# Attention weights of the differential heads turned outside TensorE, in one layer of a hybrid encoder

## The reference

```python
h = rmsnorm(x, pre_g);  P = h @ w_in          # 1024 x 3328
# A: 8 query heads, 2 key/value heads, width 64, window of 128 keys, a sink per head, ALiBi
# B: 4 heads, each with two softmax maps over keys of width 64, values of width 128
for i in range(8):                            # query blocks of 128
    s = q[i] @ k[: i + 1].T / 8 - slope * dist      # both maps, masked by chunks of 64
    p = softmax(s);  attn = p[0] - lam * p[1]
    o[i] = attn @ v[: i + 1]
o = rmsnorm(o, subln_g) * (1 - lambda_init)
y = concat(A * silu(gA), B * silu(gB)) @ w_out
out = x + rmsnorm(y, post_g)
```

## Time and profile before

| what | value |
|---|---|
| runs of before | 507.57 us median of 3 (507.13 to 507.67) |
| profiled execution | 508.39 us, span 506.6 us |
| PE busy | 499.1 us, 99% of the span, 2724 matmuls |
| DVE, ACT, POOL busy | 282.2, 244.6, 104.0 us |
| granted TensorE clock, mean | 0.996 |
| DMA | 35.19 MB, mean 69 GB/s |

### The profile page before, as it was taken

How to read it: one execution, slowest core, us unless ns; L and a number is a source line. 1 busy time by engine, 2 the same in 40 slices (tenths; PEclk the granted TensorE clock), 3 DMA queues, 4 the chain that set the end, 5 groups by cost and what they waited for, 6 DMA issues and landing times.

```text
span 506.6 us, 7438 instructions
## 1 busy us (share of the span) xinstructions
PE 499.1 (99%) x2724; PEld 420.5 (83%) x2724; DVE 282.2 (56%) x682; ACT 244.6 (48%) x555; POOL 104.0 (21%) x131
## 2 busy tenths in 40 slices
PE   8999999999999999999999999999999999999995
PEld 7999988888888888888887777788888888888884
DVE  3969743565656555455467576654763593333432
ACT  6952643555545546546466665633652462222211
POOL 1070522223032022203034335312303000000000
PEclk9999999999999999999999999999999999999998
DMA  8910141120151012211011130111000925322222
GB/s 277 308 50 0 43 123 41 25 59 0 43 124 44 1 43 55 71 42 42 1 42 43 42 85 1 42 43 41 2 1 0 251 82 155 136 83 85 83 85 82
DMA packets 43701, 35.19 MB, mean 69 GB/s; under 512 B 19025, under 2 KB 36881, under 8 KB 43665
## 3 DMA queue, kind: packets, MB, share of 16 engines
q1 hardware_dynamic: 41216, 30.52, 21.6%
q10 hardware_dynamic: 2448, 4.20, 2.2%
HBM read 26.88 MB, written 4.19 MB: 61 GB/s over the span
## 4 chain that ended last, share of the span: by engine, by line
PE 95%; issue 2%; DMA 1%; ACT 0%; SPq 0%; DVE 0%; POOLq 0%; POOL 0%; DVEq 0%; ACTq 0%
PE proj L1282 46%; PE scores L1396 15%; PE scores L1212 8%; PE scores L1307 7%; PE banks L1329 7%; PE banks L1319 3%; PE scores L1354 2%; PE banks L1374 2%; PE banks L1362 1%; PE banks L1212 1%; PE proj L1212 1%; DMA wv_raw<-in_w_in 1%; PE banks L1338 1%; PE banks L1243 0%; PE banks L1254 0%
## 5 line engine op out<-in xcount | busy, mean ns | idle before, releaser
L702 POOL TENSOR_TENSOR w_lo<-w_raw,w_hi 128x256 fp32r<-128x256 f32 x84 | 63.5, 786 | 175.9 <-ACT w_hi L780 175.9
L1282 PE MATMUL proj<-hT_hi,w_lo 128*128 128x512 f32 x336 | 90.0, 401 | 0.0
L1282 PE MATMUL proj<-hT_hi,w_hi 128*128 128x512 f32 x336 | 89.1, 399 | 0.0
L1282 PE MATMUL proj<-hT_lo,w_hi 128*128 128x512 f32 x336 | 88.7, 400 | 0.0
L1282 PEld LDWEIGHTS proj<-hT_hi,w_hi 128*128 128x128 f32 x336 | 61.0, 188 | 12.7 <-issue 0.4
L1282 PEld LDWEIGHTS proj<-hT_hi,w_lo 128*128 128x128 f32 x336 | 60.5, 188 | 13.2 <-issue 1.9
L1282 PEld LDWEIGHTS proj<-hT_lo,w_hi 128*128 128x128 f32 x336 | 60.6, 188 | 11.8 <-issue 0.8
L1111 DVE CUSTOM_DVE_ANT_0 weights<-scores,dist_b 128x128 f32<-128x128 f32 (+7 forms) x64 | 45.9, 754 | 43.9 <-PE scores L1307 43.9
L859 ACT ACTIVATE weights<-weights,small 128x128 f32<-128x128 f32 (+7 forms) x64 | 49.0, 768 | 17.5 <-DVE small L1111 17.4
L869 ACT ACTIVATE weightsT<-banks 128x512 f32<-128x512 f32 (+3 forms) x48 | 23.6, 492 | 60.7 <-PE banks L1319 60.7
L706 POOL TENSOR_TENSOR small<-small 128x4 f32<-128x4 f32 (+2 forms) x17 | 14.1, 829 | 160.8 <-DVE small L1191 108.3
(11 more groups left out here) (126 smaller groups left out, 735.1 us busy)
## 6 DMA issues: line engine op xcount, KB each, us to landing
w_raw<-in_w_in SPq DMA_DIRECT2D x13, 512.0 KB, 3.8
w_raw<-in_w_in SPq DMA_DIRECT2D x16, 256.0 KB, 3.6
x_res<-in_x SPq DMA_DIRECT2D x8, 512.0 KB, 4.4
out<-y_out ACTq DMA_DIRECT2D x14, 256.0 KB, 2.3
x_all<-in_xT SPq DMA_DIRECT2D x6, 512.0 KB, 8.1
k_stack<-k_stack SPq DMA_DIRECT2D x12, 256.0 KB, 3.7
wo_raw<-in_w_out SPq DMA_DIRECT2D x8, 256.0 KB, 5.3
wo_raw<-in_w_out SPq DMA_DIRECT2D x4, 512.0 KB, 9.9
```

The lines of the kernel that those rows point to most:

```text
L702: nc.gpsimd.tensor_tensor(w_lo[:, n % SPLIT, k], w_raw[:, n % RAW, k], w_hi[:, n % SPLIT, k].bitcast(F32), ALU.subtract).then_inc(w_lo_rea ...
L1282: last = nc.tensor.matmul(to, w[:, slot, k, :], h[:, k, HALF * half:HALF * half + HALF], start=(p == 0 and k == first), stop=(p == PIECES ...
```

## The change

The turn of the B weights leaves PE. After `b_mix` DVE transposes the 32x32 blocks of the mixed weights in place (`b_turn`). SP writes the result to a buffer in DRAM, waits until it has landed, and reads it back in four DMAs, one for each group of 32 partitions; the DRAM layout does the rest of the turn. So that the pieces are contiguous, the keys stand in another order in scores, weights and distances: all first quarters of the key blocks, then all second ones, and so on (`by_group`); the scores' matmuls read `k_stack` in runs of 32 keys. The ACT copies and `weightsT` go; there are three buffers of mixed weights instead of two.

`b_values` has v as the stationary operand and the turned weights, in runs of 32, as the moving one; it comes two slots after the scores instead of one, and in its slot after all but two of the pieces (`AFTER_VALUES`). Its result stands turned already. ACT copies the bank to `out_B` (`b_out`); for the norm PE turns four blocks back (`b_back`), ACT squares them, DVE and POOL make the root as before. SP writes the 512 factors to DRAM (`b_spread_out`) and reads them back into all partitions (`b_spread_in`), and DVE scales `out_B` in place (`b_finish`). These stages come one slot apart; in the remaining pieces, every fourth piece.

In A, the scores of the next step come directly behind the values of the one before, in the same slot. The row of 1024 norm factors goes to DRAM and back into all partitions by two DMAs of SP, and ACT puts it in order; the diagonals and their product go. One slot is added at the end, and the last slots hold 17 pieces instead of 12, so that 14 remain behind them.

```diff
-                 + [4, 7, 7, 6, 3, 6, 5, 5] + [6, 1, 5])
-SCORES_FIRST = {1, 2, 3, 10, 11, 17, 18}
-PIECE_BETWEEN = {8, 16, 36}
-PIECE_AHEAD = {37}
+                 + [4, 7, 7, 6, 3, 6, 5, 5] + [8, 4, 3, 2])
+PIECES_AHEAD = {8: 1, 16: 1, 36: 1, 37: 1}
+AFTER_VALUES = 2
...
+            turns[n + 1] = unit[1]        # an A step
+            due[n + 2] = unit[1]          # a B unit
...
-            steps.append(("b_mix", last[1]))
+            steps += [("b_mix", last[1]), ("b_turn", last[1])]
...
+            if slot in due:
+                ahead = 1 if kind == "a" else max(1, count - AFTER_VALUES)
+                take(ahead)
+                count -= ahead
+                values(due[slot])
...
+            steps.append(("a_values", turning))
+            if kind == "a" and now + 1 < STEPS_A:
+                steps += [("a_weights", 2 * now + 1), ("a_scores", now + 1)]
...
+        for at_end in ending:
+            f, stage = at_end
+            steps += [[], [("b_back", f), ("b_square", f), ("b_root", f)], [("b_spread_out", f)],
+                      [("b_spread_in", f)], [("b_finish", f)]][stage]
+            at_end[1] += 1
...
     while at < len(pieces):
         take(1)
         vector_parts()
+        for at_end in ending:
+            f, stage = at_end
+            if at % 4 == 0:
+                steps += [...][stage]
+                at_end[1] += 1
...
             load_w(1)
+            sp.wait_ge(x_scaled, 1)
+            sp.dma_start(scales[:, :], x_scale).then_inc(scales_stored, 16)
+            sp.wait_ge(scales_stored, 16)
+            sp.dma_start(scale_spread..., scales...to_broadcast([P, SEQ])).then_inc(scales_loaded, 16)
...
+            def turn(u):
+                blocks = u % TILES + 1
+                width = GROUP * blocks
+                if u >= 2:
+                    sp.wait_ge(b_turned[u % 2], 64 * (u // 2))
+                sp.wait_ge(b_blocks_turned, u + 1)
+                sp.dma_start(turn_store[u % 2, :, :, 0:width].rearrange("g p x -> p g x"),
+                             by_group(weights_of(u), blocks)).then_inc(b_turn_stored, 16)
+                sp.wait_ge(b_turn_stored, 16 * (u + 1))
+                for g in range(4):
+                    sp.dma_start(by_group(weights_of(u)[GROUP * g:GROUP * (g + 1)], blocks),
+                                 turn_store[u % 2, g, :, 0:width].rearrange("(q k) x -> k q x", q=4)
+                                 ).then_inc(b_turned[u % 2], 16)
...
+                elif step == "b_spread_out":
+                    sp.wait_ge(b_rooted, f + 1)
+                    sp.dma_start(spread_store[:, :], rms_b).then_inc(b_spread_stored, 16)
+                elif step == "b_spread_in":
+                    sp.wait_ge(b_spread_stored, 16 * (f + 1))
+                    sp.dma_start(on_b..., spread_store...to_broadcast([P, HALF])).then_inc(b_spread, 16)
...
-            for t in range(TILES):
-                nc.vector.tensor_scalar(diagonals[:, P * t:P * t + P], ident[:, :], x_scale[:, t:t + 1], None,
-                                        ALU.mult).then_inc(diagonals_made, 1)
...
+                    nc.vector.transpose(w, w).then_inc(b_blocks_turned, 1)
...
-                        nc.tensor.matmul(scale_rows[:, cols], ones[:, :], diagonals[:, cols],
-                                         start=True, stop=True).then_inc(scale_spread, 1)
...
-                    pe.wait_ge(turned_read, turned_count("b_transpose", u, (blocks - 1) // 4))
+                    pe.wait_ge(b_turned[u % 2], 64 * (u // 2 + 1))
...
-                        last = nc.tensor.matmul(mixed[:, P * (u % 4):P * (u % 4) + P], weightsT[:, b, :],
-                                                v_sb[:, b, P * head:P * head + P],
+                        last = nc.tensor.matmul(to, v_sb[:, b, P * head:P * head + P], turned_block(u, b),
```

More of the change, by code:

```diff
@@ L34 @@
 CHUNK, HEAD_DIM = 64, 64
+GROUP = 32
 EPS = 1e-6
@@ L145, in make_schedule, with values @@
     place = {unit: n for n, unit in enumerate(order)}
-    turns = {}
+    turns, due = {}, {}
     for unit, n in place.items():
-        turns.setdefault(n + 1, []).insert(0, unit)
+        if unit[0] == "a":
+            turns[n + 1] = unit[1]
+        else:
+            due[n + 2] = unit[1]
+    def values(u):
+        steps.append(("b_values", u))
+        if u % 4 == 3:
+            steps.append(("b_out", u // 4))
+            ending.append([u // 4, 0])
+    ending = []
     steps += [("split", 0), ("split", 1)]
@@ L152, in make_schedule @@
     vector_parts()
-    for slot in range(len(order) + 3):
+    for slot in range(len(order) + 4):
         kind, now = order[slot] if slot < len(order) else (None, None)
@@ L168, in make_schedule @@
             vector_parts("store_low")
-        if finishing:
-            steps.append(("b_finish", before[1] // 4))
-        turning = sorted(turns.get(slot, []))
-        first = [("b_transpose", unit, 0) if which == "b" else ("a_transpose", 2 * unit)
-                 for which, unit in turning[:1]]
-        if kind == "b":
-            assert {("kB", now // TILES), ("qB", now // TILES)} <= set(UNITS[:at // (2 * PIECES)])
-            first.append(("b_scores", now))
-        elif kind == "a":
-            first.append(("a_scores", now))
@@ L179, in make_schedule @@
-        if slot in SCORES_FIRST:
-            first.reverse()
-        if slot in PIECE_AHEAD:
-            take(1)
-            count -= 1
-        steps += first[:1]
-        if slot in PIECE_BETWEEN and len(first) == 2:
-            take(1)
-            count -= 1
-        steps += first[1:]
-        vector_parts()
-        for n, (which, unit) in enumerate(turning):
-            if n:
-                steps.append(("b_transpose", unit, 0))
-            if which == "b" and unit % TILES >= 4:
-                if n or kind is None:
-                    take(1)
-                    count -= 1
-                steps.append(("b_transpose", unit, 1))
-            if kind == "b" and n == len(turning) - 1:
+        ahead = PIECES_AHEAD.get(slot, 0)
@@ L231, in make_schedule @@
             vector_parts("store_low")
-        if finishing:
-            steps.append(("b_finish_transpose", before[1] // 4))
+        for at_end in ending:
[3 more added lines that the diff above has]
+            at_end[1] += 1
+        ending = [at_end for at_end in ending if at_end[1] < 5]
         take(max(0, count))
@@ L1064, in _ @@
                     if kind == "gB":
-                        dve.wait_ge(turned_read, turned_count("b_finish_transpose", 2 * head + half))
+                        dve.wait_ge(b_finished, 2 * head + half + 1)
                     else:
```

250 lines of the change are left out of this document (131 added, 119 removed).

## The result

The changed kernel takes 522.81 us (median of 4 runs, 521.67 to 523.01), the kernel before beside it 507.62 (4 runs, 507.13 to 507.98); ratio 1.0299, 95% interval 1.0286 to 1.0312. The profiled execution took 522.7 us with a span of 520.9. Forecast were 509.4 us, range 497 to 522. The direction was the likelier one of the two, the size was not: 15 us are lost, 2 were forecast, and the time lies 0.8 us above the range.

The account below looks back on a forecast made before the run. PE was taken as the bound, busy 499.1 of 506.6 us. From the profiled 508.4 us, less 18.4, plus 10.7, 0.5, 7.0 and 2.0, came 510.2, or 509.4 us after 0.8 off for the median; range 497 to 522.

Parts of the forecast that it names:

- the clock: PE at 1.2 GHz behind waits of 5 and 7 us: 2 us in all, between 0 and 6.
- the moves of the keys: At a head's start, key moves share time with the turn of a 512 KB unit: 0.5 us, 0 to 2.
- the start of the trips: SP's turns start behind loads at units 0, 10, 18; units 1, 9, 17 near their limit, together 0.4 us.
- work that PE loses: 144 turns, 16.7 us, and the product with the diagonals, 1.72 us, leave PE: together 18.4 us.
- waits for turned weights: PE waits for round trips before values: 5.0, 0.9, 1.8, 2.6 us at units 0, 2, 10, 18; sum 10.7.
- before the output projection: w_out's load stands behind the last bank's factors, so PE waits 7.0 us for slabs; low 2, high 9.5.
- The fourth rival: Strided operands in scores and values slow PE by 3 us; counted within the forecast's own chance of 0.44.
- the length of one trip: Write, reaction and four reads of a short unit: 7.4 us, between 6.0 and 9.9; 8.1 behind a load.
- SP is held by a load until ...: SP reaches a turn only after the load waiting for POOL's low weights: until 99.79 at unit 0, 162.02 at unit 10.
- The second rival: w_out's load comes in time, by faster slabs or an earlier last root: 503.6 us, chance 0.10.
- The third rival: SP becomes the bound in the short slots and falls behind: about 519 us, chance 0.20.
- Its sign: PE waits before most short units would show that SP bounds the short slots.

Follow-up runs that it names:

- no_trip_gap: Changed kernel without the DRAM trip (output not the reference's), w_out slabs 0 to 3 at the last values, 4 to 7 once the last factors are back: 499.20 us.
- scale_alone: Kernel before with only the norm-factor row sent through DRAM instead of PE's product with the diagonals: 505.81 us.
- load_behind: Changed kernel with weight loads that a trip follows within 12 steps issued after that trip's reads: 515.3 us.
- best3: Changed kernel with loads behind trips, root late except groups 4, 5, 7, w_out slabs earlier, mixes of units 9, 17 ahead of query-store low halves: 505.17 us.
- root_late: Changed kernel with the root of B's sums one stage later than the squares: loses 3.7 us.
- no_trip: Changed kernel without the trip through DRAM, DVE's block transposes kept, so the output is not the reference's: 503.01 us.
- both: Changed kernel with root_late's and load_behind's edits together: level with load_behind, 0.4 us above the expected 512 to 515 us.
- no_trip_wo: no_trip with slabs 0 to 5 of w_out loaded as soon as the last values are done: no gain, 3.7 us above no_trip_gap.
- fill: Changed kernel with idle identity matmuls before five units' values and the output projection, so that PE does not stand: 523.59 us.
- best_v1: both plus slabs 0 to 5 of w_out earlier, root at its old place for groups 5 and 7, values one piece later: 0.7 us gained by the last, intervals overlapping.

## Why the prediction was wrong

The prediction failed in three terms of its sum: the clock (2.0 us, with 6 as the upper bound, against 8.8), the moves of the keys (0.5, against 4.8 with what stands beside them) and the start of the trips (units 8, 9 and 16 at next to nothing, against 4.1 us). Behind the last two is one step: each trip was followed from the one load ahead of it, and not through the whole lists that SP and DVE work off before it.

The sum had five terms. The first column is the forecast's, the second is measured in the profiled execution of the kernel after; the clock is 489.9 less no_trip_gap's 481.1 us.

```
                                          forecast  measured
work that PE loses (481.1 - 499.1)           -18.4     -18.0
waits for turned weights                      10.7      13.5
key store, moved keys, ACT's squares           0.5       4.8
before the output projection                   7.0       5.9
clock                                          2.0       8.8
sum                                            1.8      15.0
```

With the two small waits of the kernel before, 0.7 us in all, that are gone as well, this is the 14.3 us by which the spans differ.

**Right: what PE loses.** The turns and the product with the diagonals are 18.0 of the forecast 18.4 us, and scale_alone shows the product's share and that its replacement through DRAM comes in time. The fourth rival is out: with strided operands and the full clock PE's whole work takes 481.1 us, 0.4 more than 499.1 less the forecast 18.4.

**Right in the sum, by two errors that cancel: the length of one trip.** From the issue of the write until PE has the values it is 6.6 us at unit 0 (97.15 to 103.70), 7.2 at unit 10 (168.94 to 176.11) and 7.8 at unit 18 (227.09 to 234.86), against 8.1 as forecast. The write takes 3.5 of them at unit 0 (3.9 and 4.5 for the three blocks of units 10 and 18), where a load was issued just before, and 1.8 where none was (load_behind, 93.39 to 95.18); I had 2.4 and 0.7 for the load. From the first read's issue to PE's start it is 3.0 to 3.3 us, where I had 4.9: reads too long and writes too short. That part is luck. The rule of the Trainium skill (DMA: Bandwidth & Descriptors, "Anatomy of one DMA — SWDGE (gpsimd) path"), stated for another issuing path, 2.0 us and the bytes at 436 GB/s, gives an estimated 2.2 us for these 64 KB: the undisturbed write agrees with it within 0.4 us, the one behind a load takes 1.7 more, and that is the case in this kernel.

**Wrong: which trips are late, and by whom.** Units 0, 10 and 18 wait as forecast (3.5, 1.9, 3.8 against 5.0, 1.8, 2.6; unit 2 not at all), but units 8, 9 and 16 bring 4.1 us that the forecast had at 0.4. The step that failed is "SP is held by a load until ...": it gave the start of a trip by POOL's low weights and SP's one load alone, and took the other units to have time enough. What the traces of the kernel after show ahead of the trips:

- Unit 0: as forecast, POOL's low weights and the load; DVE had turned at 93.4, and SP writes at 97.15.
- Units 8 and 16: SP itself. DVE has turned unit 8's weights at 148.1, but SP is at unit 7's trip until 151.35, then at a load and at the factors' way back, and writes at 153.56, 5.5 us late (rows above). At unit 16 it is 5.0 us (209.1 and 214.06).
- Unit 9: DVE. It waits 6.0 us for ACT's part of a query store, turns until 162.35, and SP writes at once, at 162.42. With that out of the way, SP is late (best3).
- Units 10 and 18: DVE, POOL and the load, and then the write behind that load (3.9 and 4.5 us). For unit 18:

```profile
147.75 0.31 DVE L1141 STREAM_TRANSPOSE weights<-weights 128x128 f32<-128x128 f32 x1
...
223.70 0.69 DVE L1171 TENSOR_REDUCE small<-on_b 128x4 f32<-128x512 f32 x1 [2.42 <-ACT on_b L935]
...
225.80 0.58 DVE L1141 STREAM_TRANSPOSE weights<-weights 128x384 f32<-128x384 f32 x1
```

```profile
224.81 1.01 POOL L768 TENSOR_TENSOR small<-small 128x4 f32<-128x4 f32 x1 [2.89 <-DVE small L1177]
225.79 0.74 POOL L764 TENSOR_TENSOR w_lo<-w_raw,w_hi 128x256 fp32r<-128x256 f32 x1
```

The first row is unit 8's turn. At unit 18 DVE's reduction waits until 223.70 and passes the delay to POOL's root, the root to the low weights, these to SP's load at 226.60, and the load to the write at 227.09; DVE itself had turned the weights at 226.4. The root's place is worth little there: in root_late, which moves it away, DVE turns at 226.5 and SP writes at 226.56, only 0.5 us earlier.

**Wrong: key store.** I counted the moves of keys (0.5 us) but not that DVE stores the new keys' low halves behind the root's sums, the mix and now the turn of a seven-block unit (1.11 us): 3.2 us in two waits. They stand in no_trip too, and are gone in both (though not in load_behind, which leaves the root in its place).

**Right in the mechanism, and short of the last step: w_out.** The load is issued 10.7 us before the last piece ends (409.01; the forecast had 10.4), ACT waits for slabs, and PE waits 5.9 us before the output projection, whose first 16 matmuls take 6.1 us instead of 3.8, most of it at half the clock. But the slabs were not alone: load them earlier and the last group's finish, its factors queued with the slabs, holds the output projection for as long (no_trip_wo). The second rival, w_out's load in time, was therefore not to be had by the load alone.

**Wrong by the most: the clock.** 2.0 us with 6 as the upper bound, 8.8 measured. The forecast had two stretches at 1.2 GHz in mind, without their length, behind waits of 5 and 7 us; the trace shows four, of 3.4 to 6.9 us, and two of them are with waits of 1.9 and 3.8 us. It is not a term that can be won back by itself, though: fill took it away and the time stayed, load_behind took unit 0's wait away and the clock came back with it.

**The third rival** (SP as the bound in the short slots, 519 us, chance 0.20) comes nearest to what happened: one change of SP's order alone is worth 7.5 us, and best3 ends with SP as the last cause at unit 9. It was to decide when one turn holds SP longer than about 5 us. From the write's issue to the end of the last read's that is 5.3, 6.5, 5.8, 5.7 and 6.3 us at units 0, 2, 8, 10 and 18, where a load stands ahead, and 3.8 and 3.7 at units 1 and 9, where none does. Its sign, waits before most short units, is there too: six of the nine units of one to three blocks wait. So this rival's mechanism is at work in part of the slots, and the forecast's sum had taken its limit as just not reached (4.9 us).

## What to carry to other kernels

A DMA round trip on the critical path is priced by its length and by everything ahead of it in the lists of each engine that hands it on: here moving ten loads from ahead of a trip to behind it gained 7.5 us. Put what is awaited soon ahead of what is awaited late in an in-order queue, and leave large transfers out from between a small one and its answer. Most of PE's waits of 2 to 6 us here came with some us at half the clock. So look at each wait and at the clock behind it, and not at the sum of one kind of wait: root_late has less of the kind that it was made for, and is slower.

## What was not expected of the hardware

With single waits of 3.5, 1.9, 3.8 and 5.9 us PE was granted 1.2 GHz for 3.4 to 6.9 us, while waits of 1.25, 1.57 and 2.38 us in the same execution were not followed by it; in root_late 2.3 us were. So the length of the single wait does not decide it here, and what does stays open. A write of 64 KB to DRAM in pieces of 128 bytes takes 1.8 us alone, and 3.5 and 4.7 us in two executions behind a load of 512 KB. Factors of 2 KB took 7.7 us to land behind six slabs of 512 KB. DVE's transpose in 32x32 blocks takes 0.31 us for 128 columns, 0.58 for 384 and 1.11 for 896. Kernels with the trips in them scatter more than those without: best_v1 from 505.4 to 511.9 us over 12 runs, load_behind from 514.1 to 518.5 over 4, no_trip_gap from 498.7 to 499.3 over 4; why one execution's trips land later than another's stays open.
